# Sixteen blocks of neighbourhood attention: maxima taken and bias added in PSUM, normalisation moved behind the values, values with queries as rows and turned back

## The reference

```python
def qkv_heads(h, w_qkv, q_g, k_g):
    q, k, v = jnp.split(h @ w_qkv, 3, axis=-1)
    return rms_norm_2(_heads(q), q_g), rms_norm_2(_heads(k), k_g), _heads(v)

def neighbourhood_attention(q, k, v, k_c, v_c, rpb):
    ...
    scale = d ** -0.5
    s_loc = jnp.einsum('bhrqd,bhrikd->bhrqik', qg, kg).astype(jnp.float32) * scale + bias
    s_loc = jnp.where(col_mask[:, None, :], s_loc, NEG_INF)
    s_ctx = jnp.einsum('bhrqd,bhcd->bhrqc', qg, k_c).astype(jnp.float32) * scale
    s = jnp.concatenate([s_loc.reshape(B_, H, rows, GRID_W, n_loc), s_ctx], axis=-1)
    p = jax.nn.softmax(s, axis=-1).astype(v.dtype)
    ...
    o = jnp.einsum('bhrqik,bhrikd->bhrqd', p_loc, vg) + jnp.einsum('bhrqc,bhcd->bhrqd', p_ctx, v_c)
```

## Time and profile before

| | |
|---|---|
| three runs | 1769.03, 1772.07, 1773.03 us, median 1772.07 |
| profiled execution | 1772.83 us, span 1771.0 us |
| mean granted TensorE clock | 0.969 |
| TensorE, weight load, VectorE, ScalarE busy | 95%, 83%, 56%, 42% of the span |

### The profile page before, as it was taken

How to read it: one execution, slowest core, us unless ns; L and a number is a source line. 1 busy time by engine, 2 the same in 40 slices (tenths; PEclk the granted TensorE clock), 3 DMA queues, 4 the chain that set the end, 5 groups by cost and what they waited for, 6 DMA issues and landing times.

```text
span 1771.0 us, 29417 instructions
## 1 busy us (share of the span) xinstructions
PE 1677.8 (95%) x11903; PEld 1469.2 (83%) x11903; DVE 999.2 (56%) x1209; ACT 751.0 (42%) x1104; POOL 91.1 (5%) x70
## 2 busy tenths in 40 slices
PE   6999999999999999779989999999979998789998
PEld 6998998989999989777767888888858874589998
DVE  6777556558785565553356443443352328776664
ACT  5545544445445544453234322233242324555453
POOL 0110000001100000020011000000020102110000
PEclk9999999999999999879999999999979998989999
DMA  7675665766665657512122323332324322045654
GB/s 250 224 232 198 203 212 191 239 221 199 233 211 198 210 173 246 199 38 82 48 72 75 92 82 100 115 90 68 93 72 149 94 83 46 20 139 169 202 175 122
DMA packets 329969, 259.69 MB, mean 147 GB/s; under 512 B 24017, under 2 KB 322385, under 8 KB 329826
## 3 DMA queue, kind: packets, MB, share of 16 engines
q1 hardware_dynamic: 311184, 251.55, 44.2%
q10 hardware_dynamic: 18642, 6.18, 1.7%
HBM read 256.65 MB, written 1.05 MB: 146 GB/s over the span
## 4 chain that ended last, share of the span: by engine, by line
PE 82%; DVE 9%; ACT 5%; issue 2%; DMA 1%; POOL 1%; ACTq 0%; SPq 0%; DVEq 0%
PE banks_g L1018 40%; PE banks_g L768 20%; PE banks_g L758 4%; PE banks_g L1006 3%; PE banks_g L790 2%; PE bank_s L885 1%; ACT near_p L1592 1%; PE banks_g L750 1%; ACT w_hi L1223 1%; PE bank_m L804 1%; DVE near_p L2012 1%; DVE near_max L2179 1%; DVE w_lo L1731 1%; PE bank_t L898 1%; POOL h L1670 1%
## 5 line engine op out<-in xcount | busy, mean ns | idle before, releaser
L1018 PE MATMUL banks_g<-h_hi,w_lo 128*128 128x512 f32 (+1 forms) x864 | 299.9, 347 | 9.7 <-DVE h_lo L2115 9.7
L1018 PE MATMUL banks_g<-h_hi,w_hi 128*128 128x512 f32 (+1 forms) x864 | 297.9, 345 | 0.0
L1018 PE MATMUL banks_g<-h_lo,w_hi 128*128 128x512 f32 (+1 forms) x864 | 297.9, 345 | 0.0
L1985 DVE TENSOR_TENSOR w_lo<-raw,w_hi 128x2048 fp32r<-128x2048 f32 (+1 forms) x100 | 208.0, 2080 | 158.8 <-ACT w_hi L1386 158.7
L1731 DVE TENSOR_TENSOR w_lo<-raw,w_hi 128x2048 fp32r<-128x2048 f32 x92 | 210.7, 2290 | 94.9 <-ACT w_hi L1223 94.7
L768 PE MATMUL banks_g<-h_hi,w_lo 128*128 128x256 f32 x800 | 227.9, 285 | 0.0
L768 PE MATMUL banks_g<-h_hi,w_hi 128*128 128x256 f32 x800 | 223.3, 279 | 0.0
L768 PE MATMUL banks_g<-h_lo,w_hi 128*128 128x256 f32 x800 | 223.2, 279 | 0.0
L1386 ACT ACTIVATE w_hi<-raw 128x2048 fp32r<-128x2048 f32 (+1 forms) x100 | 173.3, 1733 | 74.3 <-DMA raw<-w_down 48.1
L1018 PEld LDWEIGHTS banks_g<-h_hi,w_lo 128*128 128x128 f32 x864 | 164.5, 190 | 33.6 <-DVE h_lo L2115 12.0
L1223 ACT ACTIVATE w_hi<-raw 128x2048 fp32r<-128x2048 f32 x96 | 183.0, 1906 | 6.9 <-DMA raw<-even_in 2.6
(11 more groups left out here) (313 smaller groups left out, 2948.3 us busy)
## 6 DMA issues: line engine op xcount, KB each, us to landing
raw<-w_in SPq DMA_DIRECT2D x76, 1024.0 KB, 4.9
ada_raw<-ada_w SPq DMA_DIRECT2D x48, 1024.0 KB, 7.2
raw<-w_up SPq DMA_DIRECT2D x88, 512.0 KB, 4.5
raw<-w_down SPq DMA_DIRECT2D x32, 704.0 KB, 4.4
raw<-w_branch SPq DMA_DIRECT2D x12, 1024.0 KB, 4.9
raw<-qkv SPq DMA_DIRECT2D x12, 1024.0 KB, 4.9
raw<-w_out SPq DMA_DIRECT2D x8, 1024.0 KB, 5.1
raw<-even_in SPq DMA_DIRECT2D x6, 1024.0 KB, 5.2
```

What stands on the lines that cost most here:

```text
L1018: last = nc.tensor.matmul(gb[:, m * SEQ:m * SEQ + nt], w[:, c, m0:m0 + P], a[:, c, 0:nt], start=c == 0 and n == 0, stop=c == kcs - 1 and n ...
L1985: nc.vector.tensor_tensor(w_lo[:, u % SLOTS, 0:n], raw[:, u % SLOTS, 0:n], w_hi[:, u % SLOTS, 0:n].bitcast(F32), ALU.subtract).then_inc(dv ...
```

## The change

Scores are no longer copied out of PSUM. The scale 1/8 moves into the queries: their root is now taken of the sum of squares plus 64 times epsilon, in place of the mean plus epsilon. VectorE adds the bias to the first 256 columns in PSUM and takes the maxima from PSUM. ScalarE's exponentials read PSUM and write `near_p`. A block's scores banks are thus free only when its exponentials are done. The probabilities stay unnormalised. Turned, they are now the weights (128x128), and `v_n` is streamed with 64 columns for each head, so the values come with queries as rows. VectorE multiplies them by the reciprocals of the sums into `near_o`. A new step, "near back", four blocks after the scores, transposes `near_o` into another part of the same bank, from which the high and low parts are taken as before.

```diff
--- before.py
+++ after.py
@@ -323,12 +323,14 @@
         for i in range(4):
             order.append(("unit", kind, i))
             order += between.get(f"{kind}{i}", [])
-    for b in range(19):
+    for b in range(20):
         if b < 16:
             order.append(("near scores", b))
         if 2 <= b <= 17:
             order.append(("near turn", b - 2))
-        if b >= 3:
+        if b >= 4:
+            order.append(("near back", b - 4))
+        if 3 <= b <= 18:
             order.append(("near values", b - 3))
         if b < 16:
             order.append(("near exp", b))
@@ -398,6 +400,7 @@
         mod = sb("mod", [P, DEPTH, 48, 2])
         s_cols = sb("s_cols", [P, KC, 32])
         eps = sb("eps", [P, 1])
+        eps_hd = sb("eps_hd", [P, 1])
         x_t = sb("x_t", [P, KC, SEQ])
         base = at[0]
@@ -504,7 +507,8 @@
         window = sb("window", [P, SEQ], offset=f_lo_at + 16384)
         near_max = sb("near_max", [P, 2, 2], offset=f_lo_at + 18432)
         near_sum = sb("near_sum", [P, 2, 2], offset=f_lo_at + 18464)
-        near_inv = sb("near_inv", [P, 2], offset=f_lo_at + 18496)
+        near_inv = sb("near_inv", [P, 4, 2], offset=f_lo_at + 18496)
+        near_o = sb("near_o", [P, 2, P], offset=f_lo_at + 18560)
         near_p = [sb(f"near_p{n}", [P, 2, 512], offset=h2_hi_at + 4096 * n) for n in range(3)]
         near_pt = sb("near_pt", [P, 2, 4, 2, P], offset=h2_hi_at + 12288)
         bias = [sb(f"bias{n}", [P, 4, SEQ], offset=c_t_at + 4096 * n if n < 2 else h2_hi_at + 20480)
@@ -1123,7 +1127,7 @@
                         pe.wait_ge(act_steps, act_.at(f"empty{END_JOBS[('nv', 3, 1)]}"))
                     if b >= 2:
-                        pe.wait_ge(dve_steps, dve_.at(f"near masked{b - 2}"))
+                        pe.wait_ge(act_steps, act_.at(f"near exp{b - 2}"))
                     for e in range(2):
                         r = slice(64 * e, 64 * e + 64)
                         last = nc.tensor.matmul(near_banks(b)[:, e, :], q_n[r, c, qt * P:qt * P + P], k_n[r, c, :],
@@ -1131,7 +1135,7 @@
                     last.then_inc(pe_steps, pe_.step(f"near scores{b}"))
                 elif what == "near turn":
                     b, = arg
-                    pe.wait_ge(dve_steps, dve_.at(f"near probs{b}"))
+                    pe.wait_ge(act_steps, act_.at(f"near exp{b}"))
                     for hf in range(2):
                         if b:
                             pe.wait_ge(act_steps, act_.at(f"near turned{b - 1} {hf}"))
@@ -1148,12 +1152,18 @@
                     if b >= 2:
                         pe.wait_ge(dve_steps, dve_.at(f"near lo{b - 2}"))
                     ob = bank_o if b % 2 == 0 else bank_g[0]
-                    for kt in range(4):
-                        for e in range(2):
-                            hh = 2 * c + e
-                            last = nc.tensor.matmul(ob[64 * e:64 * e + 64, 0:P], v_n[:, kt, hh * HD:hh * HD + HD],
-                                                    near_pt[:, b % 2, kt, e, :], start=kt == 0, stop=kt == 3)
+                    for e in range(2):
+                        hh = 2 * c + e
+                        for kt in range(4):
+                            last = nc.tensor.matmul(ob[:, 64 * e:64 * e + 64], near_pt[:, b % 2, kt, e, :],
+                                                    v_n[:, kt, hh * HD:hh * HD + HD], start=kt == 0, stop=kt == 3)
                     last.then_inc(pe_steps, pe_.step(f"near values{b}"))
+                elif what == "near back":
+                    b, = arg
+                    pe.wait_ge(dve_steps, dve_.at(f"near o{b}"))
+                    ob = bank_o if b % 2 == 0 else bank_g[0]
+                    nc.tensor.transpose(ob[:, P:2 * P], near_o[:, b % 2, :], ident[:, :]).then_inc(
+                        pe_steps, pe_.step(f"near back{b}"))
                 elif what == "finish":
                     pe.wait_ge(dve_steps, dve_.at(f"empty{len(END_JOBS) - 1}"))
                     for b in range(4):
@@ -1573,8 +1583,9 @@
                     if half:
                         nt = SEQ if x == "q" else 512
                         act.wait_ge(pe_steps, pe_.at(f"sumsq{x}1"))
-                        nc.scalar.activation(m_root[0:16, 0:nt], bank_m[0:16, 0:nt], ACT.Sqrt, scale=1.0 / HD,
-                                             bias=eps[0:16, 0:1]).then_inc(act_steps, act_.step(f"root{x}"))
+                        by, e_ = (1.0, eps_hd) if x == "q" else (1.0 / HD, eps)
+                        nc.scalar.activation(m_root[0:16, 0:nt], bank_m[0:16, 0:nt], ACT.Sqrt, scale=by,
+                                             bias=e_[0:16, 0:1]).then_inc(act_steps, act_.step(f"root{x}"))
                 elif what == "qk spread":
                     x, = arg
                     if x == "k":
@@ -1588,8 +1599,11 @@
                         act.wait_ge(dve_steps, dve_.at(f"near masked{b - 1}"))
                         load_bias(b // 2 + 2)
                     act.wait_ge(dve_steps, dve_.at(f"near max{b}"))
+                    if b >= 3:
+
+                        act.wait_ge(pe_steps, pe_.at(f"near turn{b - 3} 1"))
                     for e in range(2):
-                        nc.scalar.activation(near_p[b % 3][:, e, :], near_p[b % 3][:, e, :], ACT.Exp,
+                        nc.scalar.activation(near_p[b % 3][:, e, :], near_banks(b)[:, e, :], ACT.Exp,
                                              bias=near_max[:, b % 2, e:e + 1], accum_out=near_sum[:, b % 2, e:e + 1]
                                              ).then_inc(act_steps, act_.step(f"near exp{b}"))
                 elif what == "near turn":
@@ -1600,14 +1614,14 @@
                         nc.scalar.activation(near_pt[:, b % 2, 2 * hf:2 * hf + 2, :, :].rearrange(
                             "p k e q -> p (k e) q"), src, ACT.Copy).then_inc(act_steps,
                                                                              act_.step(f"near turned{b} {hf}"))
-                elif what == "near values":
+                elif what == "near back":
                     b, = arg
                     qt, c = divmod(b, KC)
-                    act.wait_ge(pe_steps, pe_.at(f"near values{b}"))
+                    act.wait_ge(pe_steps, pe_.at(f"near back{b}"))
                     ob = bank_o if b % 2 == 0 else bank_g[0]
                     nc.scalar.activation(
                         f_hi[:, 0:4, :].rearrange("p a (b t) -> p (a b) t", b=2)[:, c, qt * P:qt * P + P],
-                        ob[:, 0:P], ACT.Copy).then_inc(act_steps, act_.step(f"near hi{b}"))
+                        ob[:, P:2 * P], ACT.Copy).then_inc(act_steps, act_.step(f"near hi{b}"))
                 elif what == "finish":
                     for b in range(4):
                         t, c4 = divmod(b, 2)
@@ -1622,6 +1636,7 @@
             enter("start")
             pool.sem_inc(pool_steps, pool_.total("layer") or 1)
             nc.gpsimd.memset(eps[:, :], EPS).then_inc(pool_steps, pool_.step("eps"))
+            nc.gpsimd.memset(eps_hd[:, :], EPS * HD).then_inc(pool_steps, pool_.step("eps"))
             nc.gpsimd.memset(ones[:, :], 1.0).then_inc(pool_steps, pool_.step("ones"))
             nc.gpsimd.memset(logf[:, :, :], 0.0).then_inc(pool_steps, pool_.step("logf"))
             nc.gpsimd.memset(s_cols[:, :, :], 0.0).then_inc(pool_steps, pool_.step("s cols"))
@@ -2004,14 +2019,11 @@
                                         f_hi[:, i % (FC // 2), 0:n].bitcast(F32), ALU.subtract
                                         ).then_inc(dve_steps, dve_.step(f"f lo{ly} {i}"))
-            def near_normalize(b):
+            def near_reciprocal(b):
                 dve.wait_ge(act_steps, act_.at(f"near exp{b}"))
-                nc.vector.reciprocal(near_inv[:, :], near_sum[:, b % 2, :]).then_inc(dve_steps, dve_.step("near inv"))
-                own()
-                nc.vector.tensor_tensor(near_p[b % 3][:, :, :], near_p[b % 3][:, :, :],
-                                        near_inv[:, :].rearrange("p (e o) -> p e o", o=1).to_broadcast([P, 2, 512]),
-                                        ALU.mult).then_inc(dve_steps, dve_.step(f"near probs{b}"))
+                nc.vector.reciprocal(near_inv[:, b % 4, :], near_sum[:, b % 2, :]).then_inc(
+                    dve_steps, dve_.step(f"near inv{b}"))
             u = 0
             for what, *arg in END:
@@ -2164,29 +2176,36 @@
                 elif what == "near scores":
                     b, = arg
                     qt, c = divmod(b, KC)
-                    pb, sbk = near_p[b % 3], near_banks(b)
+                    sbk = near_banks(b)
                     dve.wait_ge(pool_steps, pool_.at(f"windowed{b // 2}"))
                     dve.wait_ge(pe_steps, pe_.at(f"near scores{b}"))
                     bt = bias[b // 2 % 3][:, 2 * (c % 2):2 * (c % 2) + 2, :]
-                    nc.vector.scalar_tensor_tensor(pb[:, :, 0:SEQ], sbk[:, :, 0:SEQ], SCALE, backwards(bt),
```

(24 more changed lines are left out.)

## The result

The changed kernel takes **1754.35 us** (median of 4 runs, 1753.12 to 1755.49), the kernel before 1771.84 (4 runs, 1769.03 to 1773.03). The ratio is 0.9902, 95% interval [0.989, 0.9913], so 17.5 us less. The forecast was 1767.0 with a range of 1762 to 1774: the direction was right, the size was not.

The account below looks back on a forecast made before the run. In the attention stretch, the VectorE-ScalarE ring (4.27 us a block) should yield to TensorE (4.04). Head 5.7, blocks 62.5, tail 2.0 and clock 1.7 made 71.9 against 77.6: -5.7, rounded to -5.5, so 1767.0 us, range 1762 to 1774.

Parts of the forecast that it names:

- The rest: Outside the attention blocks: the queries' root with other scale and epsilon, one more memset at the start; priced at zero.
- Everything behind shifts with it: After the attention stretch: all work starts from the last low part and moves with it.
- Head: Start of the attention stretch: two scores at half clock, the third waiting for the first exponentials; 5.7 us.
- Clock: TensorE in the head of the attention stretch: 3.4 us at half clock allowed, 1.7 us lost.
- Values: TensorE's values matmuls: 16 records at 0.111 us plus 0.12 for the change of tiling, 1.90 us a block against 1.02.
- Turn: TensorE's turn in each block: 0.93 us in place of 1.03, as work in the same full-array form follows.
- Turning back: One more 128x128 transpose on TensorE in each block: 0.15 us with its wait, between 0.11 and 0.25.
- Tail: End of the attention stretch: the last two turnings back wait for products, about 0.5 and 1.5 us, 2.0 together.
- PSUM surcharge: VectorE's add into PSUM and maxima from PSUM: no extra cost taken, add 0.68 and maxima 1.22 us.
- B: Attention blocks: some wait keeps them near 4.2 us, about 1768.9 to 1770 us; chance 0.12.
- C: Attention stretch: each further 3.4 us at half clock costs 1.7; three more take the gain away, 1772; chance 0.10.
- D: Values matmuls: weight load and streaming don't overlap, 0.166 us a record, 1780.5 us; chance 0.10.

Follow-up runs that it names:

- after_noshift: The changed kernel with both epsilons in one tile, so that no buffer moves against the kernel before: 1765.6 us, ratio 0.9952.
- pad32: The kernel before with 32 unused bytes behind the epsilon tile, so every later buffer moves and no instruction differs: 1763.3 us, ratio 0.9941.
- extra_dve: after_noshift with one more VectorE reduction of 512 elements in each block, result unused: 1767.3 us, ratio 0.998 to the kernel before.
- half_values: after_noshift with half of the values matmuls, two of four key tiles left out: 1752.3 us, ratio 0.9891 to the kernel before.
- values_rows: The kernel before with the new values form alone (queries as rows, copied out of PSUM, turned back): 1785.3 us, ratio 1.0072.
- the fastest kernel: The kernel before with bias, maxima, exponentials in PSUM, normalisation in two operations, GpSimd's additions timed, 160 unused bytes: 1733.6 us.
- psum_only: after_noshift with the old normalisation on VectorE and the old values form: 1760.8 us, ratio 0.9933 to the kernel before.

## Why the prediction was right and wrong

**The step that failed** is the last of the sum: "The rest (other scale and epsilon of the queries' root, one more [128,1] memset at the start) changes no instruction count that anything waits for: zero." I priced the epsilon tile by its memset. As an instruction it shows no cost (after_noshift has it too, and ahead of the stretch its matmuls at full clock differ from before's by 0.3 us in all), but as 32 bytes of each partition it moved every activation buffer, and that is worth 9.4 us (pad32). With it the forecast would have been 1757.6, 3.2 us off. "Everything behind shifts with it" failed in the same way: what is behind got 4.0 us faster, and what is ahead 7.5, of which 3.4 fall where one or both executions were at half clock. No rival held this case. The range, built from rivals inside the stretch alone, ended at 1762.

**The attention, by its own steps**, was right in its mechanism. Forecast -5.7; measured 77.6 - 70.5 = 7.1 in the profiled stretch, 7.1 by after_noshift. The sum came as near as it did partly by luck, as the errors below go both ways.
- The bound moved to TensorE: yes. extra_dve and half_values show it from both sides.
- Head 5.7: measured 5.8 (1456.56 to 1462.34). Scores 1.06: the same. Clock, one piece of 3.4 us: the same.
- Values 1.90: measured **1.73**. The pace was 0.108 instead of 0.111, and the 0.12 for the change of tiling before the next scores did not appear. This is the mis-sized term, -0.17 x 16 = -2.7.
- Turn 0.93: measured 1.03 (1482.72 to 1483.74), +0.10 x 16 = +1.6. The saving by the same tiling behind it did not appear.
- Turning back 0.15: measured 0.11, -0.6 in all. The product is never waited for before the tail.
- Tail 2.0: measured 2.9. The two waits forecast are there, 0.7 for the first (1523.11 to 1523.81) and 1.5 behind the last values piece. A third was missed: the turning back of block 12 has no scores ahead of it any more and waits for its product (the row with 0.45 above), 0.7 us later than without.
- With these the sum is 71.2, 0.7 over the 70.5 measured. Of this 0.3 is the three turnings back of the tail, counted twice; the other 0.4 is not accounted for, as the pieces are rounded and taken sixteen times.
- PSUM surcharge none: right (0.70 and 1.22 us). VectorE's busy time 39 was forecast, 40.8 came.

**Rivals.** B (waits) did not happen outside the tail. C, the clock, did not happen in the changed kernel's stretch, but values_rows shows that it was a real danger: at half clock, with 3.57 us idle ahead, the same values form pays 3.3 us a piece. D (dearer values) is refuted by 0.108 us a record. The rule of the Trainium skill weighed in the prediction (TensorEngine Tiling (Array Packing), section When to Use Tiling), that 64 moving columns want swapped operands and twofold tiling, holds: the tiled form takes 1.02 us and the new one 1.73 for the same products, a factor of 1.7 and not quite two, and the fastest kernel keeps the tiled form.

## What to carry to other kernels

When a change allocates anything, write down which buffers move, and compare the unchanged parts of both traces from start to start before crediting the change. Then compare the granted clock of both. An arm with the same bytes and nothing else costs one line, and here it took about half of the credit away. In a ring over two engines, look first for VectorE work on SBUF that can meet GpSimd: moving GpSimd's work under VectorE's PSUM operations took 6.8 us off the stretch of psum_only, and the normalisation could stay.
